# Moving modulation steps and one set of squares inside a hand-ordered two-block transformer kernel

## The reference

```python
def hybrid_layer(x, ...):                       # first block, twice, then a final rmsnorm
    proj = rmsnorm(x, norm_w) @ w_in
    ya = moba_attention(aq, ak, av) * silu(ag)
    yb = head_norm(retention(rotate(bq), rotate(bk), bv)) * silu(bg)
    qk = silu(causal_dwconv(concat(cq, ck), conv_w, conv_b))
    yc = head_norm(mlstm(qk..., cv, ci, cf) * sigmoid(co)) * silu(cg)
    return x + concat(ya, yb, yc) @ w_out

def second_block(x, c, ctx, c_ctx, w_ada, b_ada, ...):
    for l in range(2):
        mx = split(silu(c) @ w_ada[l] + b_ada[l], 9)      # modulation of the tokens
        mc = split(silu(c_ctx) @ w_ada[l] + b_ada[l], 9)  # modulation of the context
        x = x + 0.5 * mx[2] * swiglu(modulate(rms_norm(x, g0), mx[0], mx[1]), w_gu, w_down)
        h_ctx = ... the same with mc ...
        x = x + mx[5] * mixer(...);  x = x + 0.5 * mx[8] * swiglu(...)
    return rms_norm(x, final_g)
```

## Time and profile before

| what | before |
|---|---|
| time, median of 3 runs | 2451.07 us (2447.58 to 2455.44) |
| the profiled execution, its own time | 2455.44 us |
| its span (first to last instruction) | 2453.7 us |
| PE busy | 2310.2 us, 94% of the span |
| VectorE busy | 1592.8 us, 65% |
| ScalarE busy | 885.3 us, 36% |
| GpSimd busy | 239.3 us, 10% |
| mean granted TensorE clock | 0.978 of full speed |

### The profile page before, as it was taken

How to read it: one execution, slowest core, us unless ns; L and a number is a source line. 1 busy time by engine, 2 the same in 40 slices (tenths; PEclk the granted TensorE clock), 3 DMA queues, 4 the chain that set the end, 5 groups by cost and what they waited for, 6 DMA issues and landing times.

```text
span 2453.7 us, 33037 instructions
## 1 busy us (share of the span) xinstructions
PE 2310.2 (94%) x13198; PEld 1966.6 (80%) x13198; DVE 1592.8 (65%) x2898; ACT 885.3 (36%) x1507; POOL 239.3 (10%) x321
## 2 busy tenths in 40 slices
PE   6988988999999999899999999999999998888998
PEld 6877878988888766677888888888888887788998
DVE  5877886878877356765589866644333356776665
ACT  4344444522223334423332222332222234544443
POOL 1002001000103000012111111200000120011001
PEclk9998999999999999999999999999999999998999
DMA  7534534655653311122256665323222232244553
GB/s 265 171 121 155 171 130 134 209 190 179 217 178 117 89 59 62 56 81 89 75 201 235 206 206 206 130 83 106 95 95 95 86 120 82 89 140 146 183 187 121
DMA packets 97657, 341.31 MB, mean 139 GB/s; under 512 B 11312, under 2 KB 13488, under 8 KB 97120
## 3 DMA queue, kind: packets, MB, share of 16 engines
q1 hardware_dynamic: 74144, 254.46, 31.0%
q0 software_dynamic: 23360, 84.74, 10.7%
HBM read 338.11 MB, written 2.48 MB: 139 GB/s over the span
## 4 chain that ended last, share of the span: by engine, by line
PE 74%; DVE 15%; ACT 5%; issue 5%; POOL 1%; DMA 0%; POOLq 0%; DVEq 0%; ACTq 0%
PE PS L547 72%; DVE WL L1214 4%; ACT WH L914 2%; DVE CV L1223 1%; PE PS L851 1%; ACT P L915 1%; DVE HL L1223 1%; DVE NT L1223 1%; DVE P L1218 1%; DVE JK L1224 1%; DVE AR L1224 1%; POOL ACC L1803 1%; DVE PJB L1223 1%; ACT PT L914 1%; DVE ST L1227 0%
## 5 line engine op out<-in xcount | busy, mean ns | idle before, releaser
L914 ACT ACTIVATE WH<-RAW 128x1024 fp32r<-128x1024 f32 (+3 forms) x498 | 511.6, 1028 | 1009.6 <-PE PS L547 1008.0
L547 PE MATMUL PS<-HH,WH 128*128 128x512 f32 (+1 forms) x2240 | 781.2, 349 | 13.4 <-ACT V L914 4.8
L547 PE MATMUL PS<-HL,WH 128*128 128x512 f32 (+1 forms) x2240 | 770.2, 344 | 0.0
L547 PE MATMUL PS<-HH,WL 128*128 128x512 f32 (+1 forms) x2240 | 770.0, 344 | 0.0
L1214 DVE TENSOR_TENSOR WL<-RAW,WH 128x1024 fp32r<-128x1024 f32 (+3 forms) x498 | 590.7, 1187 | 166.5 <-ACT WH L914 166.0
L547 PEld LDWEIGHTS PS<-HH,WH 128*128 128x128 f32 x2240 | 428.4, 191 | 80.7 <-issue 11.4
L547 PEld LDWEIGHTS PS<-HH,WL 128*128 128x128 f32 x2240 | 428.8, 191 | 52.8
L547 PEld LDWEIGHTS PS<-HL,WH 128*128 128x128 f32 x2240 | 429.2, 192 | 51.5
L547 PE MATMUL PS<-GH,WH 128*128 128x512 f32 (+1 forms) x776 | 271.1, 349 | 0.3 <-DVE WL L1214 0.3
L547 PE MATMUL PS<-GL,WH 128*128 128x512 f32 (+1 forms) x776 | 270.1, 348 | 0.0
L547 PE MATMUL PS<-GH,WL 128*128 128x512 f32 (+1 forms) x776 | 270.1, 348 | 0.0
(11 more groups left out here) (220 smaller groups left out, 2814.1 us busy)
## 6 DMA issues: line engine op xcount, KB each, us to landing
RAW<-in_wst SPq DMA_DIRECT2D x436, 512.0 KB, 3.5
AR<-in_w_adaT POOLq DMA_DIRECT2D x144, 512.0 KB, 3.8
RAW<-in_wst SPq DMA_DIRECT2D x48, 384.0 KB, 3.0
BM<-rpb_rows POOLq DMA_DIRECT2D x48, 64.0 KB, 3.0
CB<-in_cc POOLq DMA_DIRECT2D x2, 1024.0 KB, 10.7
RAW<-in_wst SPq DMA_DIRECT2D x8, 256.0 KB, 2.7
RAW<-in_wst SPq DMA_DIRECT2D x4, 396.0 KB, 3.1
rpb_rows<-in_rpb POOLq DMA_DIRECT2D x2, 697.5 KB, 11.4
```

The lines of the kernel that those rows point to most:

```text
L547: return e.matmul(o, l, r, start=start, stop=stop)
L914: return e.activation(o, i, f, bias=bias, scale=scale)
```

## The change

1. Five E's more are put into the stretch of the mLSTM's convolution of each layer (`mix(D=8, M=8, E=6)` for `E=1`), and one more into the next stretch of layer 0 (7 for 6). They are taken from layer 0's last stretch (three), from the start of layer 1 (two), from the part of the first feed-forward half that runs over the tokens alone (five) and from the rest of it (48 become 47). The count stays 73. JK1 is used for 25 rows of `w_ada` instead of 19.
2. Norm (3, C) is placed later: its first two steps behind the first and second pair of dense steps, none of its eight row steps ahead of attention step 3, all eight of them between steps 3 and 4.
3. The eight squares of norm (3, X) and the five additions stand in one piece at the start of that norm, which itself begins one dense step later. Norm (2, X) uses PSUM bank 6 instead of 7.

```diff
-        order += mix(D=7, E=2) if l else mix(D=7)
+        order += mix(D=7)
...
-        order += mix(D=8, M=8, E=1)
+        order += mix(D=8, M=8, E=6)
...
-        order += mix(D=12, M=14, T=15, E=7 if l else 6)
+        order += mix(D=12, M=14, T=15, E=7)
...
-            order += mix(D=2, E=1) + heads(5, 1)
+            order += mix(D=2) + heads(5, 1)
             pairs("w_out", l, 0, 4, "o0", "Y1", l, 0, 256)
-            order += mix(D=4, E=2)
+            order += mix(D=4)
...
-    order += ["N"]
     pairs("w_out", 1, 4, 4, "o1", "Y1", 1, 4, 256, 0, 1)
     order += ["D", "D", "N"]
     pairs("w_out", 1, 4, 4, "o1", "Y1", 1, 4, 256, 2, 1)
-    order += ["D", "N", "N", "D", "N", "N"] + heads(3, 1)
+    order += ["D", "D", "N"] + heads(3, 1)
     pairs("w_out", 1, 4, 4, "o1", "Y1", 1, 4, 256, 4, 2)
-    order += ["D", "N", "N", "D", "N", "N", "D", "D"] + heads(4, 1)
-    first = hidden(0, 0, "1", 0, 2)
+    order += ["D", "N", "N", "D", "N", "N", "D", "N", "N", "D", "N", "N"] + heads(4, 1)
+    first = hidden(0, 0, "1", *PARTS[0][0][:1], 4 // 2)
...
     order += ["D", "N", "N", "D", "N", "N"] * 2
+    order += ["D", "D"]
     order += ["D", "D", "N"]
     order += ["D", "D", "N"]
     order += ["D", "N", "D", "N"] + ["D", "N", "D", "N", "N"] * 2
-    order += ["D"] * 6
+    order += ["D"] * 4
...
-        out = mix(D=alone, E=5) if alone else []
+        out = mix(D=alone) if alone else []
...
-    nw = 72 + 1 - 25
+    nw = 72 + 1 - 26
...
-        return 3 if (j, s) == (3, C_) else 7 if j == 2 else 6 + s
+        return 3 if (j, s) == (3, C_) else 6 + s
...
-                if j == 0:
+                if j in (0, 3) and s == X_:
                     for i in range(8):
-                        if i % 4 == 0:
+                        if j == 0 and i % 4 == 0:
                             q.wait_ge(d_x[i // 4], 16)
+                        if j and not s:
+                            q.wait_ge(*vn.at("x", 2, i))
                         square(j, i, (s,))
...
-                    if j == 2:
-                        q.wait_ge(*vn.at("x", 2, k))
-                        square(3, k, (X_,))
...
-                            stt((JK1 if l == 0 and x < 19 else JK)[:, :], A, 0.5, CB[:, 1, :], ALU.mult, ALU.mult, M[:, 2 * k + 1:2 * k + 2])
+                            stt((JK1 if l == 0 and x < 25 else JK)[:, :], A, 0.5, CB[:, 1, :], ALU.mult, ALU.mult, M[:, 2 * k + 1:2 * k + 2])
...
-                if j == 0:
+                if j in (0, 3) and s == X_:
                     for i in range(1, 6):
                         add(j, i, (s,))
```

More of the change, by code:

```diff
@@ L1849, in norm @@
                 tt(SM[:, 8 + o:10 + o], SM[:, o:o + 2], MHALF[:, 0:2], ALU.pow).then_inc(*gn.inc("pow", j, s))
-                yield
-                yield
-                for k in range(8):
-                    if j == 2:
-                        add(3, k, (X_,))
+                for _ in range(10):
                     yield
```

## The result

The changed kernel is slower by more than was forecast: 2475.8 us median (2469.16 to 2478.72, 6 runs) against 2451.94 us (2447.58 to 2455.44, 6 runs), ratio 1.0093 with a 95% interval of 1.0076 to 1.011, so +23 us (+19 to +27). The forecast was +13 us, 2464, with a range up to 2474. The profiled execution of the changed kernel took 2474.52 us, with a span of 2472.7 us.

The account below looks back on a forecast made before the run. VectorE was taken to set the pace in the first block's convolutions, TensorE wherever it is fed. Terms 8.7 + 7.8 - 1.9 - 3.5 + 0 + 2.0 = +13.1 us on the 2451.07 median gave 2464, range 2450 to 2474.

Parts of the forecast that it names:

- the term of norm (3, X): At the closing matmuls after the block of squares, TensorE waits 3.2 us where it waited 1.2: +2.0 us.
- VectorE sets the pace in the fronts, an E costs its 2.29 us: Convolution stretches of layers 0 and 1: each E between groups lengthens VectorE's period to 6.23 us; TensorE late 8.7 and 7.8.
- The fifth E behind the diagonals costs nothing, the clock nothing: Layer 0 convolution: fifth E falls when VectorE has three weight tiles of lead, 0 us; no clock loss in the sum.
- reserve: Time from the end of diagonals `MI` until TensorE took them up, used first: 1.6 us in layer 0, 1.4 in layer 1.
- slow clock rival: TensorE's clock stays low behind gaps: about 2.5 us more in each convolution stretch, 1 at the seam; +19, 2470; chance 0.18.
- Second diagonals of layer 0, -1.9: At 105.75 us TensorE's 1.86 us wait for layer 0's second diagonals goes, the E ahead being moved: -1.9 us.
- End of layer 0, -3.5: Three E's leave the end of layer 0, shortening TensorE's waits for `X` and additions of squares: -3.5 us.
- Norm (3, C), 0: Around attention step 3, the wait for `X` nearly goes and the wait for `P` grows by the same: 0 us.
- the fronts would be absorbed: Rival: TensorE has more lead in both convolution stretches, only the excess over two steps is lost: +2.9 us, 2454; chance 0.20.
- the seams win: Rival: waits gone at layer ends, norm (3, X) and second diagonals give -11.7 us and decide the sign; sum -5.4, 2446; chance 0.12.

Follow-up runs that it names:

- p1_e_moves: Kernel before with part 1 of the change alone, the moves of the E steps: +12.0 us, ratio 1.0049.
- front0_only: Kernel before with six E's for one in layer 0's convolution stretch alone, the five taken from the long rest behind: +8.3 us, ratio 1.0034.
- after_spread: Changed kernel with the squares and additions of norm (3, X) spread over norm (2, X) again, bank 7: +12.0 us against the kernel before, ratio 1.0049.
- front1_only: Kernel before with six E's for one in layer 1's convolution stretch alone, the five taken from the long rest behind: +6.1 us, ratio 1.0025.
- e_behind: Kernel before with part 1, but both layers' added convolution E's put behind the diagonals, in the next stretch: +12.0 us, ratio 1.0049.
- p2_ctx_norm: Kernel before with part 2 alone, norm (3, C) placed later: +0.5 us, ratio 1.0002.
- p23_norms: Kernel before with parts 2 and 3 alone, the two norms at the seam: +11.5 us, ratio 1.0047.
- p3_both: Kernel before with part 3 alone and whole, block and later start of norm (3, X) together: +7.6 us, ratio 1.0031.

## Why the prediction was wrong

The direction, the places and the signs of the terms were right; the sum was short by ten microseconds and the range by two. What failed was the term of norm (3, X) (point 6), and the clock, which the sum put at nothing (points 2 and 6).

1. *VectorE sets the pace in the fronts, an E costs its 2.29 us.* Right: period forecast 6.23, seen 6.22 us; waits of 0.9 to 5.5 us for `WL`; the fronts alone give +8.3 and +6.1, forecast 8.7 and 7.8.
2. *The fifth E behind the diagonals costs nothing, the clock nothing.* In layer 1 TensorE took up the diagonals 8.4 us late, by reserve, as forecast, with 0.45 us for a modulation vector that I had not counted; the lag then grew to 9.9. Behind the wait of 2.77 us the seven matmuls that follow ran at the low clock for 1.5 us more than before. This is the slow clock rival. In layer 0 the changed kernel's profile does not have it: TensorE is 8.2 us late at the diagonals and 8.3 behind them. But that is luck of one profile. The other three profiles with six E's in layer 0's front (p1_e_moves, front0_only, after_spread) are 8.4 to 8.7 us late at the same diagonals and 10.1 to 10.4 behind them. The changed kernel, then p1_e_moves:

```profile
72.00:82.00 10.00, 8.89 (x50) 7.57 (x51) 9.83 (x29) 4.77 (x8) 1.14 (x2) 1.00 0.79 252
```

```profile
72.00:82.00 10.00, 8.69 (x35) 6.77 (x36) 8.69 (x22) 4.45 (x7) 1.05 (x2) 0.83 0.74 231
```

   In layer 1 it is p1_e_moves that keeps the clock (1.00 from 270 to 278 us, against 0.79) and its step is 8.3, where the changed kernel, front1_only and after_spread have 9.9. So the reserve gives 8.3 to 8.5 us in each front, near the forecast, and the clock 1.5 to 1.7 us more in three of four profiles. The fifth E behind the diagonals cost nothing, as forecast.
3. *Second diagonals of layer 0, -1.9.* The wait went, but only 0.7 was kept, the rest being lost again up to 136 us. e_behind shows that the stretch behind is as tight on VectorE.
4. *End of layer 0, -3.5.* The lag fell by 4.7 us there in the changed kernel, 2.5 us were measured alone: between the two.
   Together part 1: forecast 8.7 + 7.8 - 1.9 - 3.5 = +11.1, measured +12.0.
5. *Norm (3, C), 0.* +0.5 measured. The step inside failed: the wait for `X` did not go, since two `NT` and an `HL` still stand ahead of the split. The wait that went in p2_ctx_norm was the one at 364.41 (in the changed kernel 0.8 us of it is left). The sum came out within the bounds.
6. *Norm (3, X), +2.0.* **This is the step that failed most.** I let the block start when the step that ended at 420.5 was evicted, and had TensorE busy with one more step beside it. The block is queued behind the eviction of that later step itself, so no step lies beside it: a wait of 5.9 us instead of 3.2. And I took its after-effect as nothing: the clock from 440 to 448 us was 0.56. The two waits for `WL` behind it stayed, as forecast (1.6 and 1.7 us). Part 3 alone measured +7.6.

Of the 10 us that were missing, part 1 has 1 and parts 2 and 3 have 9.5 (measured 11.5 for 2.0), each within some 4 us. The lag steps account for 6 of them: 2.8 at norm (3, X), 1.6 at norm (3, C), 2.1 in layer 1's front, 1.2 at the second diagonals, less 1.2 at the end of layer 0 and 0.4 in layer 0's front. The other 4 us are the distance between the lag of 19.2 and the time of +23. No step of the lag up to 470 us holds them: the profiled execution of before, which the lag is taken against, was 3.5 us above its median (the 2.0 us of low clock at 424 us may be part of it); and behind 800 us the clock falls in every profile, at varying places (before, 1200 to 1250 us, 0.93; the changed kernel, 0.97 there). Whether the changed kernel sits systematically at the slow side there was not settled.

That the fronts would be absorbed or the seams win is out by p1_e_moves and p23_norms. The slow clock rival at 2470 was the nearest, and its 0.18 too little.

## What to carry to other kernels

- The idle share of an engine is not slack. VectorE stood idle 8.5 of 39 us, 4.3 of it in waits for TensorE, and yet five or six E's put there cost 60% to 75% of their length; one taken out in front of a wait gave back more than its length at that place.
- For work put into one block, ask behind which eviction it is queued and how many steps lie between there and the one who waits. One step of distance was worth 3.9 us, the block's length next to nothing.
- To place a change in a hand-ordered program, follow the lag of one repeated operation through both traces: within a pair of traces it told the steps to a few tenths of a microsecond, where the medians carry 3 to 4. But one pair holds one state of the clock: the same step in another profile differed by up to 2 us, so that more than one profile is needed.

## What the runs showed of the hardware

The granted clock made a gap on TensorE dearer than itself: behind waits of 5.9 us it was 0.50 for 4 us (the changed kernel 444 to 448 us, p3_both 432 to 436), about 2 us more in the lag. Behind shorter waits it varied from one profile to the next at the same place: behind 2.5 to 3.3 us for the diagonals it fell in six of eight cases and cost 1.5 to 1.7 us, and at one and the same wait of 1.2 us the kernel before fell to 0.50 for 4 us, and p1_e_moves did not. With the wait of 3.2 us in layer 0's front cut to 0.4, the clock stayed at 1.00. GpSimd's additions in the block came 0.87 us apart (ScalarE's squares from 440.29 to 443.75 are four such periods): they, not ScalarE's 0.42 us squares, set the block's length.
